# Two experts instead of one enter by one-hot products, and four engines share the last additions

## The reference

```python
e_in_group = jnp.take_along_axis(e_logits, g_idx[:, :, None], axis=1)[:, 0]
top_l, top_i = lax.top_k(e_in_group, TOP_K)              # 2 of 8 in the best of 4 groups
gates = g_p * jax.nn.softmax(top_l, axis=-1)
...
def expert_block(args):
    xb, e = args
    return (jax.nn.silu(xb @ w_gate[e]) * (xb @ w_up[e])) @ w_down[e]
...
out = jnp.zeros((t, d), F32).at[tok_buf].add(y_buf.astype(F32) * w_buf[:, None])
...
return rmsnorm(h, final_norm)
```

## Time and profile before

| What | Value |
|---|---|
| Median of 3 runs | 2071.75 us (2071.66 to 2072.22) |
| Profiled execution, first to last instruction (its span) | 2068.1 us |
| PE busy | 2005.8 us (97%) |
| DVE, ACT, POOL busy | 1576.0, 1338.0, 277.5 us |
| Mean granted TensorE clock | 0.995 of full |
| HBM read, written | 495.05 MB, 50.86 MB |

### The profile page before, as it was taken

The page is one execution under the profiler, slowest core; times in us unless marked ns, Lnnn a source line. Parts: engine busy times, 40 slices in busy tenths (PEclk is TensorE's granted clock), DMA queues, the critical chain, the costliest instruction groups (busy, mean ns, idle before and its releaser), DMA issues. The chain is left out here.

```text
span 2068.1 us, 29817 instructions
## 1 busy us (share of the span) xinstructions
PE 2005.8 (97%) x10448; PEld 1636.6 (79%) x10448; DVE 1576.0 (76%) x1878; ACT 1338.0 (65%) x1818; POOL 277.5 (13%) x345
## 2 busy tenths in 40 slices
PE   7999998998999999999998989999899999999998
PEld 6888876887788888888886866777688888888885
...
DMA packets 123487, 513.24 MB, mean 248 GB/s; under 512 B 27373, under 2 KB 28490, under 8 KB 89610
## 3 DMA queue, kind: packets, MB, share of 16 engines
...
HBM read 495.05 MB, written 50.86 MB: 264 GB/s over the span
## 5 line engine op out<-in xcount | busy, mean ns | idle before, releaser
L517 DVE TENSOR_TENSOR exp_w_lo<-ring_raw,first_w_hi 128x2048 fp32r<-128x2048 f32 x192 | 438.8, 2287 | 32.7 <-ACT first_w_hi L444 32.6
L517 DVE TENSOR_TENSOR exp_w_lo<-ring_raw,exp_w_hi 128x2048 fp32r<-128x2048 f32 x192 | 439.3, 2290 | 27.8 <-ACT exp_w_hi L444 27.7
L444 ACT ACTIVATE exp_w_hi<-ring_raw 128x2048 fp32r<-128x2048 f32 x192 | 367.8, 1918 | 60.4 <-PE exp_up_out L369 32.5
L444 ACT ACTIVATE first_w_hi<-ring_raw 128x2048 fp32r<-128x2048 f32 x188 | 360.5, 1918 | 60.9 <-PE exp_up_out L369 30.1
L314 POOL DMA_INDIRECT y_rows<-exp_y,base_rows_y x63 | 79.0, 1254 | 947.2 <-ACT exp_y L464 934.0
L369 PE MATMUL exp_gate_out<-exp_w_lo,exp_x_hi 128*128 128x512 f32 x512 | 199.8, 390 | 0.0
L369 PE MATMUL exp_y_out<-exp_w_lo,exp_hid_hi 128*128 128x512 f32 x512 | 199.6, 390 | 0.0
L369 PE MATMUL exp_up_out<-exp_w_lo,exp_x_hi 128*128 128x512 f32 x512 | 199.2, 389 | 0.0
L369 PE MATMUL exp_gate_out<-first_w_hi,exp_x_hi 128*128 128x512 f32 x272 | 109.3, 402 | 3.1 <-issue 2.0
L521 DVE TENSOR_TENSOR exp_x_lo<-exp_x_turned,exp_x_hi 128x1024 fp32r<-128x1024 f32 x62 | 75.9, 1224 | 47.6 <-ACT exp_x_hi L448 47.6
L369 PEld LDWEIGHTS exp_up_out<-exp_w_lo,exp_x_hi 128*128 128x128 f32 x512 | 96.1, 188 | 19.8
...
## 6 DMA issues: line engine op xcount, KB each, us to landing
ring_raw<-in_expert_w_gate_dram SPq DMA_DIRECT2D x128, 1024.0 KB, 10.9
ring_raw<-in_expert_w_up_dram SPq DMA_DIRECT2D x128, 1024.0 KB, 11.4
ring_raw<-in_expert_w_down_dram SPq DMA_DIRECT2D x128, 1024.0 KB, 11.3
...
finish_y<-y_rows SPq DMA_DIRECT2D x8, 1024.0 KB, 12.7
...
```

The lines of the kernel that those rows point to most:

```text
L444: nc.scalar.activation(split[split_slot(unit)][0][:], raw[raw_slot(unit)][:], ACT.Copy).then_inc(hi_ready, 1)
L517: nc.vector.tensor_tensor(lo[:], raw[raw_slot(unit)][:], hi[:].bitcast(F32), ALU.subtract).then_inc(lo_ready[split_slot(unit)], 1)
```

## The change

Only layer 1's experts and `finish` change, and the routing's late mark.

- Experts 30 and 31 (`kept` = 2) enter by one-hot products. Expert 30's result stays in PSUM, is scaled and split into `kept_hi` and `kept_lo` parts, and isn't scattered; expert 31's down product goes to the PSUM of `x_turned`. POOL makes the one-hots. Zeros are scattered for both experts at the start.
- The slot weights come through DRAM: POOL stores `weight` to `w_rows` and gathers 4 bytes per slot, twice. The spreading product, its diagonals, the eight one-hots and the reduction on DVE go.
- `R.late` is made for the first tile alone.
- SP waits for the scatters up to expert 29 before it loads y_rows. Tile 0 goes to another place in SBUF, and final_norm's row is loaded between tiles 6 and 7.
- The tiles are taken in the order 0, 2, 1, 3, 4, 5, 6, 7. PE adds one row of tiles 0, 2 and 7; DVE the other row of these and both of 4 and 6; of tiles 1, 3 and 5 ACT scales both rows and POOL adds them to h. Tiles 3 and 5 are normed by ACT (scale) and POOL (gain).
- Tile 0's product by PE and row by DVE, the diagonals, the table of the root, and tile 1's scaling by ACT stand ahead of the last down product. 14 transposes ahead of that product and 14 behind it go.

The core of the diff:

```diff
-    dve.drain()
-    v.tensor_scalar(R.late[:, :, t], R.block_hot[:, :, 0, N_EXPERTS - 1].bitcast(F32), 0.0, None, ALU.not_equal)
+    if t == 0:
+        dve.drain()
+        v.tensor_scalar(R.late[:], R.block_hot[:, :, 0, N_EXPERTS - 1].bitcast(F32), 0.0, None, ALU.not_equal)
...
+        y_last = x_turned[:].rearrange("p k n -> p (k n)") if weighted else y_out[:]
+        hots = [hot, x_hi]
+        row_parts = [(last_hi, last_lo), kept_rows]
...
+            def make_hot(pool, j):
+                for t in range(8):
+                    nc.gpsimd.tensor_scalar(hots[j][:, t], c["iota"][:], tokens[:, j, t:t + 1], None, ALU.is_equal).then_inc(hot_made, 1)
...
-            pool.indirect_dma_start(y_rows, bass.IndirectOffsetOnAxis(ap=rows_y[:, E - 1:E], axis=0), y[1][:], None,
-                                    bounds_check=2047, oob_is_err=False).then_inc(scattered[1], 16)
+            for e in range(E - kept, E):
+                pool.indirect_dma_start(y_rows, bass.IndirectOffsetOnAxis(ap=rows_y[:, e:e + 1], axis=0), y[1][:], None,
+                                        bounds_check=2047, oob_is_err=False).then_inc(scattered[1], 16)
...
+                if weighted and e == 1:
+                    pool.wait_ge(weighed, 1)
+                    pool.dma_start(w_rows.rearrange("(p c) n -> p (c n)", p=P), weight[:].rearrange("p k t -> p (k t)")).then_inc(weights_stored, 16)
+                    make_hot(pool, 0)
+                if weighted and e == 2:
+                    pool.wait_ge(weights_stored, 16)
+                    for j in range(kept):
+                        pool.indirect_dma_start(w_slot[:, j:j + 1], None, w_rows, bass.IndirectOffsetOnAxis(ap=w_at[:, j:j + 1], axis=0),
+                                                bounds_check=2047, oob_is_err=False).then_inc(weights_taken, 16)
+            if weighted:
+                until_last_unit(pool, 3)
+                make_hot(pool, 1)
...
-            for k in range(14):
-                nc.tensor.transpose(x_turned[:, k % 4], c["ident"][:], c["ident"][:])
-            down_of(E - 1, (last_pair, 6))
+            if weighted:
+                after.tensor_early(pe)
+            else:
+                for k in range(14):
+                    nc.tensor.transpose(x_turned[:, k % 4], c["ident"][:], c["ident"][:])
+            down_of(E - 1, (last_pair, 6), y_last)
...
-            copy_y(E - 2, 0, (last_pair, 5))
-            hid_high(E - 1)
+            if weighted:
+                after.scalar_first(act)
+                hid_high(E - 1)
+                until_rows_stored(act)
+                act.wait_ge(weights_taken, 16 * kept)
+                for cols in row_halves:
+                    nc.scalar.activation(row_parts[1][0][:, cols], y_out[:, cols], ACT.Copy, scale=w_slot[:, 0:1]).then_inc(kept_hi_made, 1)
+            else:
+                copy_y(E - 2, 0, (last_pair, 5))
+                hid_high(E - 1)
             after.scalar_early(act)
             act.wait_ge(unit_done, done_count((last_pair, 7)))
...
-                v.tensor_tensor(last_parts[:].rearrange("p (t n) -> p t n", t=8), bc(c["ident"][:], 1, 8), bc(w_last[:], 2, P), ALU.mult)\
-                    .then_inc(diag_made, 1)
...
-            for t in range(tiles):
-                v.tensor_scalar(hot[:, t], c["iota"][:], tokens[:, t:t + 1], None, ALU.is_equal)
-            if weighted:
-                dve.wait_ge(spread, 1)
-                dve.drain()
-                v.tensor_tensor(last_parts[:], hot[:].bitcast(F32).rearrange("p t n -> p (t n)"), y_out[:], ALU.mult).then_inc(y_copied, 1)
-                dve.drain()
-                v.tensor_reduce(w_slot[:], last_parts[:], AX.X, ALU.add)
...
+            if weighted:
+                after.vector_first(dve)
             hid_low(E - 1)
+            if weighted:
+                for half, cols in enumerate(row_halves):
+                    dve.wait_ge(kept_hi_made, half + 1)
+                    v.scalar_tensor_tensor(row_parts[1][1][:, cols], y_out[:, cols], w_slot[:, 0:1], row_parts[1][0][:, cols].bitcast(F32),
+                                           ALU.mult, ALU.subtract).then_inc(kept_made, 1)
             after.vector_early(dve)
...
+        def until_kept_rows(engine):
+            engine.wait_ge(hot_made, 8 * kept)
+            engine.wait_ge(kept_made, 2)
+        def multiply_kept(t, outs, first):
+            for out, cols in zip(outs, row_halves):
+                for n, part in enumerate(row_parts[1]):
+                    last = nc.tensor.matmul(out, hots[1][:, t], part[:, cols], start=(first and n == 0), stop=False)
+            return last
+        def until_rows_turned(engine):
+            engine.wait_ge(x_turned_s, E)
         def until_rows_stored(engine):
-            engine.wait_ge(scattered[0], 16 * (E // 2))
-            engine.wait_ge(scattered[1], 16 * (E // 2))
+            engine.wait_ge(scattered[0], 16 * ((E - kept + 1) // 2))
+            engine.wait_ge(scattered[1], 16 * (E // 2) + (16 if weighted else 0))
...
-    T, ACC, both = 8, 4, (2, 4, 6)
+    T, ACC = 8, 4
+    order = (0, 2, 1, 3, 4, 5, 6, 7)
+    by_tensor, by_pool, pool_norms = (0, 2, 7), (1, 3, 5), (3, 5)
+    place = {t: n for n, t in enumerate(order)}
...
+            before.until_rows_turned(sp)
             for t in range(T):
-                if t < 6:
-                    before.until_slot_read(sp, t)
+                if 1 <= t < 7:
+                    before.until_slot_read(sp, t - 1)
+                if t == 7:
+                    before.until_last_unit(sp, 4)
+                    sp.dma_start(gain[:], broadcast_row(A["final_norm"], P)).then_inc(gain_ready, 16)
                 sp.dma_start(y[t][:], y_rows[256 * t:256 * t + 256, :].rearrange("(p k) d -> p k d", k=2)).then_inc(y_ready[t], 16)
-            for t in range(T):
-                sp.wait_ge(made, t + 1)
+            for t in order:
+                until_made(sp, t)
                 sp.dma_start(out[0, t * P:(t + 1) * P, :], h[:, t]).then_inc(stored, 16)
...
+            for n, t in enumerate(by_pool):
+                for k in range(2):
+                    pool.wait_ge(row_scaled, 2 * n + k + 1)
+                    nc.gpsimd.tensor_tensor(h[:, t], h[:, t], y[t][:, k], ALU.add).then_inc(row_added, 1)
+                    pool.drain()
+            pool.wait_ge(gain_ready, 16)
+            for n, t in enumerate(pool_norms):
+                pool.wait_ge(half_normed, n + 1)
+                nc.gpsimd.tensor_tensor(h[:, t], h[:, t], gain[:], ALU.mult).then_inc(pool_made, 1)
+        def row_product(pe, t, first):
+            n = by_tensor.index(t)
+            pe.wait_ge(diag_made, n + 1)
+            pe.wait_ge(y_ready[t], 16)
+            for b, half in enumerate(halves_of(t)):
+                nc.tensor.matmul(half, diag[:, n], y[t][:, 1, b * BANK:(b + 1) * BANK], start=first, stop=False)
+        def tensor_early(pe):
+            row_product(pe, order[0], True)
         def tensor(pe):
...
+            for n, t in enumerate(order):
...
+                if n >= ACC:
+                    pe.wait_ge(combined, n - ACC + 1)
+                if n == 0:
+                    before.until_kept_rows(pe)
+                before.multiply_kept(t, halves_of(t), n > 1)
+                if n == 0:
+                    row_product(pe, order[1], True)
                     before.until_last_rows(pe)
-                before.multiply_last(t, [acc[t % ACC][:, 0:BANK], acc[t % ACC][:, BANK:]], False).then_inc(summed, 1)
-            for t in range(T):
-                rows(t)
-                last_rows(t)
-        def scalar_early(act):
-            before.until_last_unit(act, 5)
-            for t in range(T):
-                for k in (0, 1) if t in both else (1,):
-                    last = nc.scalar.activation(diag[:, t, k], c["ident"][:], ACT.Copy, scale=weight[:, k, t:t + 1])
-            last.then_inc(diag_made, 1)
+                if n > 1 and t in by_tensor:
+                    row_product(pe, t, False)
+                before.multiply_last(t, halves_of(t), False).then_inc(summed, 1)
...
+        def scalar_first(act):
+            before.until_last_unit(act, 3)
+            for n, t in enumerate(by_tensor):
+                nc.scalar.activation(diag[:, n], c["ident"][:], ACT.Copy, scale=weight[:, 1, t:t + 1]).then_inc(diag_made, 1)
             nc.scalar.activation(root[:, 0:1], c["eps"][:], ACT.Sqrt)
             act.drain()
-        def vector_early(dve):
-            pass
+            rows_for_pool(act, 1)
+        def rows_for_pool(act, t):
+            act.wait_ge(y_ready[t], 16)
+            for k in range(2):
+                nc.scalar.activation(y[t][:, k], y[t][:, k], ACT.Copy, scale=weight[:, k, t:t + 1]).then_inc(row_scaled, 1)
+        def scalar_early(act):
+            rows_for_pool(act, 3)
         def scalar(act):
...
+            def half_norm(t):
+                act.wait_ge(inverted, pool_norms.index(t) + 1)
```

(45 more changed lines are left out.)

138 lines of the change are left out of this document (60 added, 78 removed).

## The result

| | Kernel before | Changed kernel |
|---|---|---|
| Median, all runs of one chip | 2072.53 us (10 runs, 2071.66 to 2075.97) | 2078.70 us (10 runs, 2075.89 to 2081.72) |
| Ratio | 1 | 1.0025, 95% interval 1.0017 to 1.0034 |
| Repeated | 2072.99 us (19 runs) | 2075.87 us (10 runs), ratio 1.0019 (1.0009 to 1.0029) |
| Profiled execution | span 2068.1 us | span 2074.6 us, time 2076.33 us |

The change makes the kernel slower, by 0.25% (5.2 us) and in the repetition by 0.19% (3.9 us). The forecast was +2.0 us, ratio 1.0010.

The account below looks back on a forecast made before the run. PE was taken to bound the kernel, the change touching the start of layer 1's experts and the tail behind expert 29. Terms: 4.7 − 2.2 − 0.5 = +2.0, span 2070.1, time 2073.8 us; range 2068.0 to 2077.8.

Parts of the forecast that it names:

- Start of layer 1's experts, 2.2 saved: Start of layer 1's experts: spreading the slot weights leaves DVE and PE, so hid to first down product shortens by 2.2 us.
- the weight loads can follow a start that early: Layer 1's experts: weight loads keep up with the earlier start, as in layer 0, so the 2.2 us saved remain.
- rival B: Layer 1's loads do not follow the earlier start, tile 1 holds ACT 2.2 longer: +4.3, 2076.1 us; chance 0.12.
- Routing, 0.5 saved: Routing: seven of eight late marks per layer go, about 0.25 us saved per layer, 0.5 in two.
- Tail, +4.7: Behind expert 29: replaying the new order engine by engine, the end comes at 2072.8, 4.7 us later than 2068.1.
- The new wait of ACT: Ahead of the last down product: ACT stands at tile 1's load before hid's high part, making PE 2.7 us late.
- rival C: Gap ahead of the last down product: PE's clock falls to half, adding up to 5.5 us, 2076.2 in full; chance 0.1.
- The turns of POOL and DVE: Finish: POOL's additions (2.4) and DVE's rows (1.2) alternate, so the first combine starts at 2040.7, 4.1 us late.
- Outputs: Last norm to end of span: tiles 6 and 7 are stored after POOL's tile 5, 5.7 us instead of 4.3.
- B with POOL at 2.65: Loads lag behind the earlier start and POOL's additions take 2.65 us: 2077.6, given as 2077.8 for the range's upper end.
- A: Tail: first, no POOL-DVE turns (2069.7); second, earlier rows (2071.1); both 2066.3 us. Chance 0.15 of over 4.1 us faster.
- D: The one-hot entry is hidden or changes nothing; only front and routing count: 2069.1 us; chance 0.1.

Follow-up runs that it names:

- fewer_bytes: Changed kernel with layer 1 loading 768 of the 1024 columns of every second down unit, 4% fewer weight bytes; 2072.72 us, ratio 1.0000 to the kernel before.
- after_again: The changed kernel, unchanged, run and profiled a second time; 2075.87 us, ratio 1.0019 to the kernel before.
- tile1_behind: Changed kernel with tile 1's two scalings on ACT moved from ahead of hid's high part to behind expert 30's high parts; 2076.48 us, ratio 1.0018.
- pool_thin: Changed kernel with POOL's six additions and two gain multiplications on 64 of the 1024 columns, every wait kept; 2072.79 us, ratio 0.9997.
- no_pool2: Changed kernel without POOL and ACT in additions and norms, both rows of tile 4 by PE, gain loaded ahead of tile 5; 2066.70 us, ratio 0.9972.

## Why the prediction was right and where it failed

The sign and the range held: 2071.75 x 1.0025 is 2076.9, inside 2068.0 to 2077.8. But the forecast was "within 0.2%"; 0.25% is outside it, and 0.19% at its edge. That the total came out in the range is in part luck, since one term had the wrong sign and the tail's parts offset each other. By its own steps:

- **Start of layer 1's experts, 2.2 saved.** The mechanism was right, and so nearly was the size (2.4 saved at expert 3); at expert 31 it is 1.6. The step "the weight loads can follow a start that early" failed: I took it from layer 0, which has no PE wait, and left ACT's waits for loads near the end of layer 1, which the trace of before had, to rival B. B's lag is real, 0 to 2.3 us behind fewer_bytes, but not its price of 4.3: the tail is 54.2 with a lag of 1.6 (changed) and with one of 0.0 (after_again).
- **Routing, 0.5 saved.** This is the term that was off most. Layer 1's experts start 2.7 later in the mean, not 0.5 earlier. What the removed marks save can't be seen beneath it. About half of it is a load in the first 27 us that lands 1.0 to 1.5 later, which nothing in the rows of before could tell. And I charged nothing for the granted clock outside the tail, although the trace of before had its falls (0.72 in the window from 346 to 352 us); what it costs is not shown.
- **Tail, +4.7.** Measured 54.19 − 49.80 = +4.4, twice. The sum was right and its parts were not. The new wait of ACT was 2.82 plus PE's 4.06 idle, near my 2.7, but as tile1_behind shows it did not carry to the end. The clock of rival C fell, in the gap that I named, and made the product 1.9 longer; with the gap and the fall both gone (tile1_behind) the end was 0.2 earlier. The turns of POOL and DVE are as the earlier trace rows had them, and POOL's work costs 5.0 at the end, but not where I put most of it, ahead of the first combine: POOL, busy with its one-hots, began at 7.2 behind hid 31, paused for 5.66 behind its first addition, and the turns fell beside the norms. First combine at 20.4 behind hid 31 instead of 22.4, and from there to the last norm 27.9 instead of 26.4. Outputs 5.9, forecast 5.7.
- **Sum.** With what was measured: +2.7 − 1.6 + 4.4 = +5.5, against 5.2 and 3.9 timed. The forecast had −0.5 − 2.2 + 4.7 = +2.0. Two small slips stand in it: 22.1 and its waits of 4.2 make 26.3, not 26.4, and B with POOL at 2.65 is 2077.6 in one place and 2077.8 in another.
- **Rivals.** A's second half is what fewer_bytes produced by less traffic (first combine 16.5), and pool_thin its first. Together with the right order they are no_pool2. Both halves lay in the design and neither in the kernel. D did not happen: the front's 1.6 counts, and the tail is far from neutral.

The Trainium skill (SBUF — State Buffer, SBUF: two separate sides) describes the lock between GpSimd (POOL) and VectorE (DVE) as held for a whole instruction. The trace agrees for operations that read SBUF twice: 1.28 becomes 1.9 to 2.95, and pool_thin's 1.28 is the counter-test. The Trainium skill advises against idle gaps between bursts of matmuls (TensorE: Matmul & The Clock Gate, Why this matters for your kernels). The rows of 0.79 and 0.63 behind a gap of 4.06 agree with that; that the fall costs time at the end, tile1_behind does not bear out for this kernel.
